# Gated scan of a two-block hybrid model: span sums as two rounded products instead of one full-precision product

## The reference, cut to what matters

```python
f = lb + (1.0 - lb) * jax.nn.sigmoid(z)
log_f = jnp.log(jnp.maximum(f, F_FLOOR))
...
def step(state, inp):
    qb, kb, vb, lfb = inp
    b = jnp.cumsum(lfb, axis=2)
    diff = b[:, :, :, None, :] - b[:, :, None, :, :]
    decay = jnp.where(tri, jnp.exp(jnp.where(tri, diff, 0.0)), 0.0)
    attn = jnp.einsum('bhtd,bhsd,bhtsd->bhts', qb, kb, decay)
    o = jnp.einsum('bhts,bhsv->bhtv', attn, vb) + jnp.einsum('bhtd,bhdv->bhtv', qb * jnp.exp(b), state)
    b_last = b[:, :, -1:, :]
    new_state = jnp.exp(b_last[:, :, 0, :])[..., None] * state + jnp.einsum('bhsd,bhsv->bhdv', kb * jnp.exp(b_last - b), vb)
    return new_state, o
```

## Time and profile before

| | us |
|---|---|
| median of 3 runs | 5682.04 (5681.06 to 5684.04) |
| the profiled execution | 5693.57 |
| its span | 5690.7 |
| PE busy | 5217.6 (92%) |
| DVE busy | 2763.4 (49%) |
| ACT busy | 2216.1 (39%) |
| POOL busy | 376.0 (7%) |

### The profile page before, as it was taken

One profiled execution on the slowest core, in us unless ns is written; L12 is line 12 of the kernel. 1 busy time (PEld: TensorE's weight loads), 2 busy tenths in 40 slices (PEclk: granted clock), 3 DMA queues, 4 the chain that ended last, 5 costly groups with the idle time before them and its releaser, 6 DMA issues. The chain is left out here.

```text
span 5690.7 us, 97271 instructions
## 1 busy us (share of the span) xinstructions
PE 5217.6 (92%) x38308; PEld 4549.8 (80%) x38309; DVE 2763.4 (49%) x4412; ACT 2216.1 (39%) x3428; POOL 376.0 (7%) x576
## 2 busy tenths in 40 slices
PE   6895989979999899997989988999999999999994
PEld 5573977767777799997877777989898999999994
DVE  2498536432844455554146434444444555555444
ACT  2352226332444444444234423333333444444432
POOL 0123100000500000000014001000000000000001
PEclk8996999989999999998999988999999999999997
DMA  1110000221002655553100334444444554555544
GB/s 68 49 63 21 1 21 16 82 89 39 2 19 93 240 206 196 197 207 125 48 19 19 126 122 171 154 152 155 161 155 166 185 194 177 201 189 186 183 155 186
DMA packets 104465, 688.50 MB, mean 121 GB/s; under 512 B 12304, under 2 KB 16160, under 8 KB 63136
## 3 DMA queue, kind: packets, MB, share of 16 engines
q1 hardware_dynamic: 90608, 639.74, 31.2%
q0 software_dynamic: 8816, 27.44, 1.3%
q10 hardware_dynamic: 4800, 17.83, 0.8%
HBM read 622.67 MB, written 62.29 MB: 120 GB/s over the span
## 5 line engine op out<-in xcount | busy, mean ns | idle before, releaser
L3368 DVE TENSOR_TENSOR experts_low<-experts_raw,experts_high 128x1024 fp32r<-128x1024 f32 x678 | 810.6, 1223 | 1011.4 <-ACT experts_high L3297 1011.3
L3232 PE MATMUL ps<-experts_xs_high,experts_high 128*128 128x256 f32 (+1 forms) x3584 | 1038.8, 290 | 38.1 <-issue 35.4
L3232 PE MATMUL ps<-experts_xs_high,experts_low 128*128 128x256 f32 (+1 forms) x3584 | 1040.6, 290 | 3.0 <-issue 3.0
L3232 PE MATMUL ps<-experts_xs_low,experts_high 128*128 128x256 f32 (+1 forms) x3584 | 1041.1, 290 | 0.6 <-issue 0.6
L3232 PEld LDWEIGHTS ps<-experts_xs_high,experts_high 128*128 128x128 f32 x3584 | 681.4, 190 | 53.4 <-issue 44.0
L3297 ACT ACTIVATE experts_high<-experts_raw 128x1024 fp32r<-128x1024 f32 x678 | 687.7, 1049 | 31.4 <-DMA experts_raw<-experts 31.4
L3232 PEld LDWEIGHTS ps<-experts_xs_low,experts_high 128*128 128x128 f32 x3584 | 681.0, 190 | 10.3 <-issue 1.0
L3232 PEld LDWEIGHTS ps<-experts_xs_high,experts_low 128*128 128x128 f32 x3584 | 681.3, 190 | 1.2 <-issue 1.2
L2907 PE MATMUL ps<-dense_xs_parts,dense_high 128*128 128x256 f32 x2816 | 499.3, 280 | 4.3 <-DVE dense_xs_parts L3010 2.8
L2907 PEld LDWEIGHTS ps<-dense_xs_parts,dense_high 128*128 128x128 f32 x2816 | 436.8, 189 | 12.6 <-issue 5.1
L3224 PE MATMUL ps<-experts_high,experts_hid_high 128*128 128x512 f32 x1120 | 444.7, 397 | 0.0
(11 more groups left out here) (543 smaller groups left out, 9192.7 us busy)
## 6 DMA issues: line engine op xcount, KB each, us to landing
experts_raw<-experts SPq DMA_DIRECT2D x226, 1536.0 KB
dense_raw<-dense SPq DMA_DIRECT2D x90, 1536.0 KB, 6.3
mixT<-w_in SPq DMA_DIRECT2D x36, 512.0 KB
y_slot<-mla_blank SPq DMA_DIRECT2D x15, 1152.0 KB
out_proj_raw<-w_out SPq DMA_DIRECT2D x48, 256.0 KB
proj_keys_raw<-w_in SPq DMA_DIRECT2D x20, 512.0 KB
x_mixed<-mixT SPq DMA_DIRECT2D x16, 512.0 KB, 2.6
h_rows<-out_proj_rows SPq DMA_DIRECT2D x16, 512.0 KB
```

What stands on the lines that cost most here:

```text
L3232: last = nc.tensor.matmul(ps[:, m, 0:width], w[:, u, m, c], x[:, k, 0:width], start=(k == 0 and i == 0), stop=(k == KD - 1 and i == 2))
L3368: nc.vector.tensor_tensor(low[:, v, t, :], raw[:, v % NR, t, :], high[:, v, t, :].bitcast(F32), ALU.subtract).then_inc(split, 1)
```

## The change

`decay_rows` now rounds each turned block once to F32R on ACT (`log_high`, all 8 blocks), and DVE subtracts that from the turned block in PSUM and writes the rest back into `z`, over the block that was turned. It also copies the constant `spans` to an F32R tile. In `gated_chunks` the span sum of a head is two F32R products that accumulate in PSUM, high part and rest, each with the rounded `spans`. `decays` has one more axis for the two parts, and POOL fills it with four copies a chunk instead of two; it waits once per pair of copies.

```diff
-def decay_rows(core, name, z, log_decays):
+def decay_rows(core, name, z, log_high, spans):
...
-            for b in range(0, NT, 2):
+            for b in range(NT):
                 act.wait_ge(turned, b + 1)
-                nc.scalar.activation(log_decays[:, b, :], core.ps[:, b, :], ACT.Copy)
+                nc.scalar.activation(log_high[:, b, :], core.ps[:, b, :], ACT.Copy).then_inc(rounded, 1)
...
-            for b in range(1, NT, 2):
-                dve.wait_ge(turned, b + 1)
-                nc.vector.tensor_copy(log_decays[:, b, :], core.ps[:, b, :])
+            nc.vector.tensor_copy(spans[:, :], core.c("spans"))
+            for b in range(NT):
+                dve.wait_ge(rounded, b + 1)
+                nc.vector.tensor_tensor(z[:, :, b * P:(b + 1) * P], core.ps[:, b, :].rearrange("p (j n) -> p j n", j=4),
+                                        log_high[:, b, :].bitcast(F32).rearrange("p (j n) -> p j n", j=4), ALU.subtract)
...
-    decays = st.sb("decays", [P, 2, 2 * P])
+    decays = st.sb("decays", [P, 2, 2, 2 * P], F32R)
...
-                    nc.gpsimd.tensor_copy(decays[64 * m:64 * m + 64, u, :], log_decays[rows, bass.ds(i, 1), c].rearrange("p b n -> p (b n)"))\
+                    half_rows = slice(64 * m, 64 * m + 64)
+                    nc.gpsimd.tensor_copy(decays[half_rows, u, 0, :], log_high[rows, bass.ds(i, 1), c].rearrange("p b n -> p (b n)"))\
                         .then_inc(s["decays_in"], 1)
-                    pool.wait_ge(s["decays_in"], 2 * n + m + 1)
+                    nc.gpsimd.tensor_copy(decays[half_rows, u, 1, :].rearrange("p (j n) -> p j n", j=2),
+                                          oT[rows, 2 * m:2 * m + 2, bass.ds(i * P, P)]).then_inc(s["decays_in"], 1)
+                    pool.wait_ge(s["decays_in"], 4 * n + 2 * m + 2)
...
-                pe.wait_ge(s["decays_in"], 2 * n + 2)
+                pe.wait_ge(s["decays_in"], 4 * n + 4)
...
-                    last = mm(ps[:, h, :], decays[p0:p0 + 64, u, (h % 2) * P:(h % 2 + 1) * P], core.c("spans", p0, p0 + 64),
-                              start=True, stop=True)
+                    for part in range(2):
+                        last = mm(ps[:, h, :], decays[p0:p0 + 64, u, part, (h % 2) * P:(h % 2 + 1) * P], spans[p0:p0 + 64, :],
+                                  start=part == 0, stop=part == 1)
```

More of the change, by code:

```diff
@@ L2323, in inputs_and_gates @@
     st.end()
-def decay_rows(core, name, z, log_decays):
+def decay_rows(core, name, z, log_high, spans):
     nc = core.nc
     st = Stage(core, name)
-    turned = st.sem("turned")
+    turned, rounded = st.sem("turned"), st.sem("rounded")
     with nc.Block(name) as block:
@@ L2340, in _, with gated_chunks @@
         def _(act):
-            for b in range(0, NT, 2):
+            for b in range(NT):
                 act.wait_ge(turned, b + 1)
-                nc.scalar.activation(log_decays[:, b, :], core.ps[:, b, :], ACT.Copy)
+                nc.scalar.activation(log_high[:, b, :], core.ps[:, b, :], ACT.Copy).then_inc(rounded, 1)
         @block.vector
         def _(dve):
-            for b in range(1, NT, 2):
-                dve.wait_ge(turned, b + 1)
-                nc.vector.tensor_copy(log_decays[:, b, :], core.ps[:, b, :])
+            nc.vector.tensor_copy(spans[:, :], core.c("spans"))
[3 more added lines that the diff above has]
+                                        log_high[:, b, :].bitcast(F32).rearrange("p (j n) -> p j n", j=4), ALU.subtract)
     st.end()
-def gated_chunks(core, name, qk, log_decays, inputs, oT):
+def gated_chunks(core, name, qk, log_high, spans, inputs, oT):
     nc = core.nc
@@ L3545, in mix_layer @@
                 inputs_and_gates(core, f"inputs{l}", l, xT, d[f"w_hi{l}"], inputs, qk, z, mixT[:, 0:4, :])
-            log_decays = sb2("log_decays", [P, NT, HALF])
-            decay_rows(core, f"decay_rows{l}", z, log_decays)
-            gated_chunks(core, f"gated{l}", qk, log_decays, inputs, z)
+            log_high = s2.enter_context(nc.sbuf_tensor(f"log_high{l}", [P, NT, HALF], F32R))
+            spans = s2.enter_context(nc.sbuf_tensor(f"spans{l}", [P, HALF], F32R))
+            decay_rows(core, f"decay_rows{l}", z, log_high, spans)
+            gated_chunks(core, f"gated{l}", qk, log_high, spans, inputs, z)
         with ExitStack() as s2:
```

## The result

The changed kernel takes 5700.13 us (median of 13 runs, 5693.55 to 5707.74) against 5684.04 us of the kernel before on the same chip (13 runs, 5668.05 to 5691.92): ratio 1.0034, 95% interval 1.0027 to 1.0042, so 15 to 24 us slower, 19 by the ratio; the two medians themselves lie 16 us apart. The forecast was +23 us, near the upper end.

The account below looks back on a forecast made before the run. PE and POOL both bound the scan; POOL's loop grows from 6.96 to 7.91 us. Scan +9.5 and turning stage +2.0 us, times two layers, make +23 us on 5682.0: 5705 us, range 5691 to 5721.

Parts of the forecast that it names:

- Two loops of one length: Gated scan: PE's and POOL's loops per chunk both take about 6.96 us, POOL having at most 0.1 us of room.
- POOL's loop before: Gated scan, before the change: POOL's loop without foreign waits takes 6.9 to 6.96 us a chunk; 6.96 was used.
- 0.75 us for two copies: POOL in the scan: the two added decay copies lengthen each chunk's loop by 2 x 0.375 us.
- the 0.64 with a gap: POOL's added decay copies: upper-end cost of 0.64 us each, including the 0.24 us gap of a waited copy.
- Contention 0.2 us: POOL's level products running together with DVE's query factors: 0.2 us more a chunk, between 0 and 0.42.
- PE's sums 1.0 us: PE in the scan: eight F32R span-sum products take 1.0 us a chunk instead of 1.92.
- PE's wait: PE waits about 1.7 us a chunk for POOL's decay copies before the span sums, costing only idle time.
- Start, end, turning stage: Per layer: first `ends` about 0.8 us earlier, scan end 1.8 us sooner, turning of the log decays 2.0 us longer.
- (a): Rival, 12%: PE's idle time in each chunk lowers its clock; a few falls a layer cost about 16 us, 5721 us.
- (b): Rival, 5%: POOL's gaps are foreign waits, PE keeps setting the pace, each chunk saves 0.9 us; 5659 us.
- (c): Rival, 11%: POOL's added copies partly covered, no contention, loop 7.4 us; 5691 us, counted as no change.
- (d): Rival, 5%: PE's F32R products do not overlap or run no faster, sums keep 1.84 us; 5709 us.

Follow-up runs that it names:

- e1: Kernel before, each POOL decay copy followed by a second into a spare tile nobody reads; ratio to before 1.0035, loop 7.87 and 7.82 us.
- e8: Kernel before with the decay copies of chunks 2 to 15 on ACT instead of POOL; ratio to before 0.9980, repeated 0.9992.
- e2: Kernel before with one F32R product per head instead of a float32 one, rest of log decays left out; ratio to before 1.0004.
- e3: Changed kernel with the decay copies of chunks 2 to 15 on ACT instead of POOL; ratio to the kernel before 0.9981, on another chip 0.9978.
- e10: Kernel before with POOL's two decay copies of a chunk in the other order; ratio to before 1.0006, loop 7.08 and 7.05 us.
- e6: Changed kernel with the eight span-sum products reordered so neighbours use different halves of the rows; ratio to the kernel before 1.0038.
- e5: Changed kernel with one POOL wait per chunk for the four decay copies and one for the two value copies; ratio to the kernel before 1.0022.

## Why the prediction was right

- **Two loops of one length.** Shown from both sides: adding only POOL's copies costs 0.35% (e1), with POOL out of the way PE's own loop is 6.96 us (e8), with PE relieved and POOL as before the loop stays at about 7.0 us (e2, steady chunks of layer 1), and POOL's waits for others are zero in the changed kernel.
- **POOL's loop before.** I took 6.96 us as the average of two kinds of chunk; over ten steady chunks of layer 0 it is 7.01, with at most 0.1 us of that a wait for the state. The base was up to 0.05 us too low.
- **0.75 us for two copies.** Measured 2 x 0.35 = 0.70. The row of unwaited neighbours was the right one; the 0.64 with a gap was not.
- **Contention 0.2 us.** The level products take 2.87 instead of 2.65 us, half of the 0.42 from the first chunk, which would be the price in full: DVE's factors start 0.83 us after them (1509.98 - 1509.15), not with them, so the 0.42 is not paid in each chunk. Over the ten steady chunks of layer 0 POOL's starts lie 0.71 us further apart at the decay copies, 0.23 at the level and end products and 0.08 less at the value copies: +0.85, from 7.01 to 7.87. So the second price is 0.15 us net. It was forecast a little high and the base a little low, and a part of the closeness of the sum is that these errors cancel. Loop 7.91 forecast, 7.87 and 7.81 measured, so +11.6 and +11.0 for 14 loops against +12.1.
- **PE's sums 1.0 us.** Measured 1.13, and without effect.
- **PE's wait.** I put all of it, 1.7 us, before the sums. It is 0.94 there and 0.67 before the next products, where PE waits for query factors that DVE forms more slowly beside POOL. The step missed this second wait; it costs nothing, for e1 has no such wait and the same loop.
- **Start, end, turning stage.** First `ends` 14.40 us after the first transpose against 13.51, +0.9, forecast 2.0 - 0.8 = +1.2. End from the 15th `ends` to the last output copy 18.03 us against 18.96: -0.9, forecast -1.8; the first product after that `ends` comes after 4.27 us, when DVE's factors are done, and not after the 3.5 of POOL's own work. Layer sum: +0.9 + 11.6 - 0.9 = +11.6 and, in layer 1, +11.0, forecast +11.5.
- **Rivals.** (a) did not happen: the clock is 1.00 from the second loop to the end of both scans. The low stretch at the stage's start is there in both kernels: 0.50 to 0.58 from 1449.4 to 1461 us in the changed one, before 0.65 from 1452 and 0.50 from 1460.2 to 1467. In the steady chunks a fall happened in e2, where it cost one loop 0.7 us. (b) had its condition wrong, for POOL's gaps are its own, and it was priced wrong: with POOL out of the way PE's saving is 6.96 - 6.84 = 0.1 us a chunk and not 0.9, because the ring over DVE is next. I had added up each engine's work and found DVE at 6.2 us, which says nothing of a chain that passes from one engine to the other and back. (c), the copies partly covered, would give a loop of 7.4 us; the loop grew by more than the copies' 0.70 us. (d) is out: 1.13 us is less than 1.84.

What stays open: e3's scan and turning stage are 3.3 us shorter than before in the profiles, while its two ratios say 11 and 12 us. Some 8 us are won outside the stages that I read, or lie in differences between builds. Some 2 us may lie between the two scans, where this kernel's two profiles have 1368.7 and 1368.6 us, the kernel before 1370.4 and e10 1370.9. After the second scan the same kernel took 2613.5 us in one profile and 2601.0 in the other, so the profiles can't settle the rest. In the changed kernel, too, 22 us in the scans stand against 16 to 19 in the totals.

## What to carry to other kernels

An engine with 74% busy time can be the bound: add its gaps to its loop and ask whether anybody else ends them. Before an operation is made cheaper by splitting its operand, ask which engine must bring the second half, and whether that one has room. And before a gain is priced at the full saving of one engine, look for the next loop, also for rings that run over two engines.

## What the runs showed of the hardware

- Eight F32R products of 64 rows x 512 columns hold PE for 1.13 us where four float32 ones hold it for 1.92, in either order of the program (e6).
- POOL copies of 64 x 256 that follow each other without a wait are 0.35 us apart on the decay tiles. A copy of the same size takes 0.69 us where it starts together with a DVE product of two tensors, and where the copy starts 0.05 us earlier it takes 0.39 us and the DVE product 0.63 instead of 0.41 (e5 and the changed kernel).
- POOL and DVE slow each other where both take products of two tensors: 2.87 for 2.65 us on POOL, 2.92 for 1.94 us on DVE, the greater share on DVE's side. The 1.94 us are measured beside POOL's value copies.
- The granted clock at the start and the end of a stage differs between executions of one kernel: in layer 1 of e8 the second loop took 8.22 us with the clock at 0.87 in it, in the repetition 6.41 us at 1.00.
